# A fused decoder layer on eight cores: first weight slots used in turn over both chunks, and five pieces of work re-timed

## The reference

```
x = x + 1/2 * SwiGLU_1(RMSNorm(x))              # d_ff 2816: (silu(h@w1) * (h@w3)) @ w2
h = RMSNorm(x); proj = h @ w_in                 # q|k|v|gate r|decay code|pool u|ga|gb, 5648 columns
a = gated linear attention(q, k, v, decay)      # 4 heads, chunked, state dk 128 x dv 256
a = (RMSNorm per head(a) * silu(r)) @ w_up_a
b = (causal means of u over 2/4/8/16 tokens - u), 128x128 map per group, @ w_up_b
x = x + (sigmoid(ga) * a + sigmoid(gb) * b) @ w_mix_out
x = x + CrossAttention(RMSNorm(x), RMSNorm(mem))# 4 heads into 256 memory tokens
x = x + 1/2 * SwiGLU_2(RMSNorm(x))
out = RMSNorm(x)
```

## Time and profile before

| | us |
|---|---|
| median of 3 runs (lowest, highest) | 3164.24 (3163.45, 3164.89) |
| profiled execution, its own time | 3164.13 |
| span of its slowest core, core 3 | 3162.3 |
| shortest and longest core span | 3154.3, 3162.3 |
| TensorE busy | 3101.8 (98%) |
| VectorE, ScalarE, GpSimd busy | 1186.6, 950.2, 481.1 |
| DMA over the span | mean 92 GB/s |

### The profile page before, as it was taken

The page is one execution under the profiler, slowest core; times in us unless marked ns, Lnnn a source line. Parts: engine busy times, 40 slices in busy tenths (PEclk is TensorE's granted clock), DMA queues, the critical chain, the costliest instruction groups (busy, mean ns, idle before and its releaser), DMA issues.

```text
span 3162.3 us, 43137 instructions; the slowest of 8 cores (3154.3 to 3162.3 us)
## 1 busy us (share of the span) xinstructions
PE 3101.8 (98%) x15350; PEld 1448.9 (46%) x15350; DVE 1186.6 (38%) x1880; ACT 950.2 (30%) x1637; POOL 481.1 (15%) x557
## 2 busy tenths in 40 slices
PE   6999999999999999999999999999999999999998
PEld 2444454444444454444444445444444444544443
DVE  2231743621421373551332156363232226536212
ACT  3121442521211253252121135243212114425211
POOL 0002111220200220112110112012121021112002
PEclk9999999999999999999999999999999999999999
DMA  8597444335663534334384365232548345422534
GB/s 165 87 162 120 83 81 120 59 62 95 124 122 70 99 68 94 107 67 76 65 170 76 56 107 100 48 120 54 91 92 159 64 79 93 81 67 52 93 67 104
DMA packets 56784, 292.32 MB, mean 92 GB/s; under 512 B 5632, under 2 KB 11136, under 8 KB 32256
## 3 DMA queue, kind: packets, MB, share of 16 engines
q0 software_dynamic: 39024, 251.35, 44.5%
q1 hardware_dynamic: 17552, 38.21, 3.7%
HBM read 495.78 MB, written 22.02 MB: 164 GB/s over the span
## 4 chain that ended last, share of the span: by engine, by line
PE 94%; DVE 2%; DMA 2%; issue 1%; ACT 0%; SPq 0%; DVEq 0%; ACTq 0%; POOLq 0%; POOL 0%
PE psum_all L106 94%; DMA vo_s<-ov_mst 1%; PE psum_all L122 1%; DVE sb_hT L418 1%; DMA sb_small<-small 0%; DVE ov_nmx L1019 0%; DMA sb_slot<-ffn_w 0%; SPq L134 0%; DVE ov_Pm L1031 0%; DVE ov_pwA L733 0%; ACT ov_rstd L412 0%; DVE sb_xT L418 0%; ACT ov_rstd L410 0%; DVE ov_kT L700 0%; DVE ov_pwB L733 0%
## 5 line engine op out<-in xcount | busy, mean ns | idle before, releaser
L106 PE MATMUL psum_all<-sb_hT,sb_slot 128*128 128x512 bf16 x7680 | 1692.4, 380 | 9.0 <-DVE sb_hT L418 7.9
L106 PEld LDWEIGHTS psum_all<-sb_hT,sb_slot 128*128 128x128 bf16 x7680 | 749.8, 98 | 911.6 <-issue 23.9
L106 PE MATMUL psum_all<-ov_gated,sb_slot 128*128 128x512 bf16 x2816 | 613.2, 380 | 3.4 <-DMA sb_slot<-ffn_w 3.4
L518 DVE TENSOR_TENSOR ov_gated<-psum_all,ov_sl 128x512 bf16<-128x512 f32 x352 | 243.4, 692 | 924.0 <-PE psum_all L106 892.9
L515 ACT ACTIVATE ov_sl<-psum_all 128x512 bf16<-128x512 f32 x352 | 210.2, 597 | 902.8 <-PE psum_all L106 870.4
L106 PEld LDWEIGHTS psum_all<-ov_gated,sb_slot 128*128 128x128 bf16 x2816 | 276.0, 98 | 337.1 <-issue 6.1
L387 ACT ACTIVATE ov_sqt<-sb_xT 128x512 bf16<-128x512 f32 x224 | 140.1, 629 | 550.7 <-DVE sb_xT L539 215.8
L394 POOL TENSOR_TENSOR ov_acc<-ov_acc,ov_sqt 128x512 f32<-128x512 f32 x180 | 211.4, 1175 | 482.9 <-ACT ov_sqt L387 480.3
L134 POOL DMA_DIRECT2D sb_slot<-ffn_w x176 | 95.1, 542 | 1238.5 <-PE psum_all L106 1213.6
L106 PE MATMUL psum_all<-sb_slot,sb_hT 128*128 128x512 bf16 x1024 | 235.4, 379 | 2.6 <-DVE ov_kT L700 2.6
L418 DVE SCALAR_TENSOR_TENSOR sb_hT<-sb_xT,sb_small,ov_rstd 128x512 bf16<-128x512 f32 x192 | 141.7, 798 | 29.6 <-ACT ov_rstd L412 29.6
(11 more groups left out here) (138 smaller groups left out, 2007.7 us busy)
## 6 DMA issues: line engine op xcount, KB each, us to landing
sb_slot<-ffn_w POOLq DMA_DIRECT2D x88, 1024.0 KB, 11.2
sb_slot<-ffn_w POOLq DMA_DIRECT2D x88, 704.0 KB, 7.2
sb_slot<-w_in POOLq DMA_DIRECT2D x40, 1024.0 KB, 13.2
out<-sb_xT SPq DMA_DIRECT2D x14, 1024.0 KB, 11.9
ov_xin<-x SPq DMA_DIRECT2D x12, 1024.0 KB, 13.7
sb_slot<-w_up_a POOLq DMA_DIRECT2D x8, 1024.0 KB, 12.5
sb_slot<-w_mix_out POOLq DMA_DIRECT2D x8, 1024.0 KB, 11.2
sb_slot<-kq_s POOLq DMA_DIRECT2D x8, 1024.0 KB, 5.1
```

The source lines that it names most:

```text
L106: ("ins", (lambda e, o=o, l=l, r=r, st=st, sp=sp: e.matmul(o, l, r, start=st, stop=sp)), i == n - 1)
L518: S.op("dve", lambda e, b3=b3, slt=slt, j=j, s=s: e.tensor_tensor(out=gated[:, j, sl(s)], in0=b3[:], in1=slt[:], op=ALU.mult), [bb3, slb[0 ...
```

## The change

The staging tiles get a table of places, `MST_AT`: no tile lies at 98 or 99 any more, 55 and 56 come in, and those at 90 to 97 stand third to tenth in the order of use, not sixth to thirteenth (with 98 and 99 behind them). SP issues the constants ahead of x. The memsets of the ones matrices stand ahead of the two casts. POOL loads slot 0 once x's second piece is there, then x's second chunk with no wait, then slot 1. The memory's load waits for slot 1 and no longer for x's second chunk. In pass 1 of tile 0 the first pair is split into two single slots: chunk 0 and then chunk 1 go through slot 0, then both through slot 1, and the second chunk's norm comes after the first two column blocks, not the first four. The memory's squares come after chunk 1 of slot 1, and `mem_rest` is a step of its own that is emitted after column block 4. `pool(3 - i, 1)` takes the groups in the reverse order. In `xattn` a block's transposes stand a step later and between the two halves of a later block's scores; the last one stands behind the loop.

```diff
@@ -22,7 +22,8 @@
-NMST = 19
+MST_AT = [50, 51, 90, 91, 92, 93, 94, 95, 96, 97, 52, 53, 54, 46, 47, 48, 49, 55, 56]
+NMST = len(MST_AT)
@@ -291,7 +292,7 @@
-    mst = [ov(f"mst{i}", 50 + i if i < 5 else 85 + i if i < 15 else 31 + i, [128, 512], BF16) for i in range(NMST)]
+    mst = [ov(f"mst{i}", MST_AT[i], [128, 512], BF16) for i in range(NMST)]
@@ -350,14 +351,14 @@
         for lo in range(0, 8, step):
             S.dma(queue, [(xt[:, lo:lo + step, :], x_d[k, :, lo:lo + step, :])], after, xb[lo:lo + step], f"dma:x{queue}{k % 2}_{lo}")
 
+    S.dma("sp", [(small[:], small_d)], [], [const_b], "dma:const")
     load_chunk(0, 1)
-    S.dma("sp", [(small[:], small_d)], [], [const_b], "dma:const")
     wa_b = Buf("walpha")
     cb2 = Buf("const2")
+    S.op("dve", lambda e: e.memset(onesD[:], 1.0 / 1024.0), [], [cb2])
+    S.op("dve", lambda e: e.memset(onesV[:], 1.0 / 256.0), [], [cb2])
     S.op("dve", lambda e: e.tensor_copy(out=identB[:], in_=small[:, O_IDENT:O_IDENT + 128]), [const_b], [cb2])
     S.op("dve", lambda e: e.tensor_copy(out=triB[:], in_=small[:, O_TRI:O_TRI + 128]), [const_b], [cb2])
-    S.op("dve", lambda e: e.memset(onesD[:], 1.0 / 1024.0), [], [cb2])
-    S.op("dve", lambda e: e.memset(onesV[:], 1.0 / 256.0), [], [cb2])
     CB = [const_b, cb2]
 
     def gvec(off, kc):
@@ -492,9 +493,10 @@
     def ffn(l, x_in, hooks, nxt, between=(), drip=()):
         S.label = f"ffn{l}/p1"
         drip = list(drip)
-        pairs = [(0, 1), (2, 3), (4, 5), (6, 7), (8, 9), (10,)]
         between = list(between)
-        ahead = 0 if between else 1
+        first = len(between) > 0
+        pairs = ([(0,), (1,)] if first else [(0, 1)]) + [(2, 3), (4, 5), (6, 7), (8, 9), (10,)]
+        ahead = 0 if first else 1
         got = {}
         for pi, pair in enumerate(pairs):
             for jp in [jp for p in pairs[:pi + 1 + ahead] for jp in p]:
@@ -518,13 +520,13 @@
                         S.op("dve", lambda e, b3=b3, slt=slt, j=j, s=s: e.tensor_tensor(
                             out=gated[:, j, sl(s)], in0=b3[:], in1=slt[:], op=ALU.mult),
                             [bb3, slb[0]], [gb])
-                        if pi == 0 and s == 0 and between and j == 1:
+                        if s == 0 and j == 0 and first:
                             deferred.pop(0)()
-                        if s == 0 and j == (3 if between else 0):
+                        if s == 0 and j == (1 if first else 0):
                             run_deferred()
-                        if pi >= 1 and drip:
+                        if pi >= (2 if first else 1) and drip:
                             drip.pop(0)()
-                if (pi, s) >= (0, 1) and between:
+                if (pi, s) >= (1, 1) and between:
                     S.label = "mem"
                     between.pop(0)()
                     S.label = f"ffn{l}/p1"
@@ -917,7 +919,7 @@
             if i >= 3:
                 fill()
             if i < 4:
-                pool(i, 1)
+                pool(3 - i, 1)
             if i == 9:
                 pend["yb"] = xload(0, wpb_d, wpb_db)
                 pend["gb1"] = xload(1, win_d[10])
@@ -1056,7 +1058,10 @@
             hook(s, m + 1)
 
         for i in range(8):
-            scores_mm(i)
+            scores_mm(i, (0,))
+            if i >= 3:
+                transp(i - 3)
+            scores_mm(i, (1,))
             if i == 0:
                 S.label = "xa/dnorm"
                 n1.ones()
@@ -1067,8 +1072,7 @@
                 finish(i - 1)
             if i < 2:
                 n1.apply(4 * i, 4 * i + 4)
-            if i >= 2:
-                transp(i - 2)
+        transp(5)
         finish(7)
         ffn_pre(1)
         for m in range(8):
@@ -1084,13 +1088,14 @@
 
     S.label = "load"
     x0 = xin[0][1]
-    wpre(("ffn", 0, 0), w13_d[0][0], [xin[0][1][0]])
-    wpre(("ffn", 0, 1), w13_d[0][1], [xin[0][1][7]])
+    wpre(("ffn", 0, 0), w13_d[0][0], [xin[0][1][1]])
     load_chunk(1, 2, queue="pool")
+    wpre(("ffn", 0, 1), w13_d[0][1])
+    slot1 = pre_issued[("ffn", 0, 1)][1]
     x1 = xin[1][1]
     S.dma("pool", [(walpha[:], walpha_d), (wa[:], wa_d)], [], [wa_b], "dma:const2")
     S.dma("sp", [(pmf[:], pmix_d.rearrange("p (a b) -> p a b", a=4))], x1, pmf_b, "dma:pmf")
-    S.dma("sp", [(memT[:], mem_d)], x1, memT_b, "dma:mem")
+    S.dma("sp", [(memT[:], mem_d)], [slot1], memT_b, "dma:mem")
     n0 = first_norm(0, chain=0, raws=raw0)
     n0.sq_all()
     n0.rest()
@@ -1101,7 +1106,7 @@
         S.label = "ffn0"
         if t == 0:
             mb = mem_blocks()
-            mb = [mnorm.sq_all, lambda f=mb[0]: (mem_rest(), f())] + mb[1:]
+            mb = [mnorm.sq_all] + mb
         nx0, nx1 = xnorm(O_G_MIX, 0), xnorm(O_G_MIX, 1, chain=7)
 
         def nxt(idx):
@@ -1117,7 +1122,7 @@
         hooks = {(0, m): [lambda m=m, f=nx0: f.sq(m)] for m in range(8)}
         hooks.update({(1, m): [lambda m=m, f=nx1: f.sq(m)] for m in range(8)})
         hooks[(1, 6)].append(nx0.rest)
-        ffn(0, xin, hooks, nxt, mb if t == 0 else ())
+        ffn(0, xin, hooks, nxt, mb if t == 0 else (), [mem_rest] if t == 0 else ())
         n1 = mixer(t, nx1)
         n1 = xattn(t, n1)
         S.label = "ffn1"
```

## The result

The changed kernel takes 3143.91 us (median of five; its runs lie between 3142.49 and 3143.97) against 3164.89 for the kernel before in the same session (3163.45 to 3168.49): 21.0 us less, a ratio of 0.993 (95% interval 0.991 to 0.9945). A second session gave the same ratio, with medians of 3140.96 and 3163.0. The forecast was 3145.0. In some executions the cores of a die had a lower granted clock and took 50 us and more longer, and every range and ratio here leaves these out.

A forecast was written before the change was run, and what follows sets the result against it. TensorE, busy 98% of the span, bounds the kernel, so only its waits could be won. On core 7, 3161.7 - 6.5 - 9.4 - 3.1 + 0.5 = 3143.2, with 1.8 around it 3145.0 us; range 3139 to 3152.

The forecast's parts named there:

- start: Before and in tile 0's first matmuls: first matmul on slot 0 4.9 us earlier, plus 1.6 from pace; 6.5 less.
- memory's norm: At the first block on `mhT`: 7.2 us of TensorE idle and 2.2 of slow restart go; 9.4 less on every core.
- transposes: In `xattn`: the four waits for `Pm`, 0.9 and three times 0.7, go; 3.1 us less.
- poolings: Waits for `ogT` and `kT` in step 4 go (4.3 us), four bank waits of 1.2 come (4.8); 0.5 more.
- staging: At POOL's w2 load: core 3 gains 3.4 us plus 1.4 of slow restart, 4.8; core 7's 1.8 stays.
- The term for the pace: First eight matmuls on slot 0 come 0.43 us apart instead of 0.66: 7 x 0.23 = 1.6 us less.
- What would show it: Signs on the slowest core's trace, such as TensorE starting at 14 to 15 us and no waits for `mhT` or `Pm`.
- Rivals C: Memory's load or squares come late, so its norm still stops TensorE; 9.4 partly returns, 3150 to 3154 us; chance 0.07.
- D: Memory lands so late behind slot 1 that its ones matmuls wait; slower than before, 3165 to 3170 us; chance 0.03.
- Rival B: At the poolings: the bank wait is not met, all 4.3 us are gained, time 3140; chance 0.12.
- the sum: Core 7, forecast slowest: 3161.7 - 6.5 - 9.4 - 3.1 + 0.5 = 3143.2 us; core 3: 3139.0.
- rival A: At the start: x's last piece creeps while slot 0 streams; the start gives 0 to 1 us, 3151; chance 0.20.

The follow-up runs named there:

- the order 3, 0, 2, 1: Changed kernel with chunk 1's poolings taken as 3, 0, 2, 1, not 3, 2, 1, 0: median 3137.3 us, beside 3141.0 for the changed kernel.
- both slots first: Changed kernel with poolings 3, 0, 2, 1 and chunk 0 through slots 0 and 1 before chunk 1: median 3131.2 us, beside the changed kernel's 3141.0.

## Why the prediction was right

**The mechanism of each part held, and only sizes were off.** As differences from the kernel before by the ratios, on the slowest core: start 8.2 (forecast 6.5), memory's norm 9.5 (9.4), transposes 3.8 (3.1), poolings 0.6 less with an interval from 4 less to 2.5 more (0.5 more), staging 1.3 less with an interval from 5 less to 3 more (nothing, since core 7's wait stays). They add up to 23.4, and the whole change gave 21.0 and 22.1. The parts are thus additive to what can be told, which is not finely: each of these intervals is 6 us wide or more.

**Start, 8.2 instead of 6.5.** Both terms were too small. The first matmul came 5.5 (core 7) and 5.9 us (core 3) earlier, against 4.9. The term for the pace was 1.6, the difference of 0.66 and 0.43 over seven matmuls, as if the rest of the restart were equally slow in both kernels. It was not: only the first six matmuls come 0.43 apart now, and full clock is granted in the whole first block. From its first matmul on slot 0 to the second chunk's ones matmuls, core 3 took 18.48 us for 64 before and 8.32 for 32 now; at the warm 0.216 a matmul (10.36 for 48) that is 4.7 and 1.4 lost, so 3.3 is won. Of this 0.4 goes back in the second norm (6.39 from its ones matmuls to the restart instead of 5.95), and 0.7 in the 112 matmuls behind it, which lose 5.1 where 128 lost 4.4: after this restart the granted clock stays at half for 8.7 us, and before it was back after 7.3. 5.9 + 3.3 - 0.4 - 0.7 = 8.1. The prediction had put this second norm at nothing won or lost.

**What would show it.** TensorE's first instruction was forecast at 14 to 15 and came at 6.8 to 11.2. That was a slip, not a finding: each ones matmul waits for its own piece, so the first goes with the first square. Only the last mattered, and it ended at 14.7 on core 7. The first matmul on slot 0, forecast at 22.3, came at 21.7 to 23.2, and on the slowest core it waited for the DMA, as forecast. No wait of over 5 us appeared before 70 us but those ahead of the first block.

**Memory's norm, as forecast.** The apply of `mhT` ended at 73.91 on core 3, 3.2 us before TensorE asked for it, and no bank ran out:

```profile
69.31 4.60 DVE L419 SCALAR_TENSOR_TENSOR ov_mhT<-sb_memT,sb_small,ov_rstd 128x256 bf16<-128x256 f32 x8 [2.44 <-ACT ov_rstd L413]
```

The memory landed 14.9 us after its issue on core 7, at 50.6, where I had taken the 22.4 of the earlier trace rows and 61; the ones matmuls came at 65.6 there and at 65.8 on core 3. Rivals C and D had no part in it.

**Poolings, as forecast.** The bank was the same one: four new waits of 1.08 against the 1.2 of the prediction, 4.3 for the 4.3 that went. A shifted sum's 0.80 from start to start was the right price. Rival B asked for this wait not to be met; it is met in every tile, and the order 3, 0, 2, 1 shows what B would have given, 3.6 us.

**The slowest core: the sum was right, the core wrong.** Core 7 was to come out at 3143.2 and came out at 3134.3. It lost 18.5 by the sum, 1.7 more at the start and 0.5 at the poolings, and 4.7 of waits for loads which I had left in place: 5.3 before, the 1.8 of the earlier trace rows and four for `w_in`, of which 0.6 is left. The four, in the kernel before on that core:

```profile
PE psum_all L106 <- DMA sb_slot<-w_in: 3.5, 4, 1.1
```

With 2.0 us that no term explains that is its 27.4. The late loads now stand on core 2, and they move between executions: in the next run of the changed kernel core 2 had a span of 3132.6 and core 3 one of 3140.0. So the time of the slowest core could be forecast from core 7 as if its load waits stayed, since in each profile of the changed kernel some core loses time to late DMAs, while the core itself could not. That the number came within 1.1 us is in part luck, by two errors that cancel: core 7 gave 8.9 us more than its sum, and core 2, which stood at 3155.8 before, gave only 13.8. In the second profile it is x's late last piece on core 5, rival A on one core, that fills the place of the late loads.

## What to carry to other kernels

A saved wait at the start was worth more than its length, since the restart behind it was shorter too: let the applies run ahead while a load is still under way, and the matmuls then start in a close row. When one load is released by the arrival of another's first pieces, the margin differs from core to core and from execution to execution, so look at all cores of more than one profile. When a chain of small operations stops TensorE, look for independent work of its length and move it in between, and then check which load or buffer is waited for next; here that was worth 9.4 us at the memory's norm and 3.5 at the second chunk's. Moving elementwise work out of one step costs in the step that takes it as soon as its engine has no gap left there, so spread the long ones apart instead of bringing them all forward.

## What the hardware showed beyond this

- A few hundred nanoseconds at the start decide 8 us. With slot 0 issued at x's first piece, core 5 issues it at 6.42 and squares the last piece of x at 23.66; core 0 issues it at 6.71 and squares the last at 15.44. In between lies only whether x's 2 MB have nearly passed when POOL's packets begin to take every other turn.
- Why the granted clock fell where it did stays open. On core 3 of the changed kernel it stayed at 1.00 through the stop of 6.6 us ahead of slot 0's block, and fell inside the shorter one, which lasts from 32.8 to 36.57:

```profile
34.00:35.00 1.00, 0.00 (x0) 0.00 (x0) 0.00 (x0) 0.90 (x3) 0.00 (x0) 1.00 1.25 217
35.00:36.00 1.00, 0.00 (x0) 0.00 (x0) 0.33 (x1) 0.50 (x1) 0.00 (x0) 0.50 1.13 193
```

  It came back at 45.2. With both slots first, on core 2, it fell at 36.0, 0.3 us after a restart in a close row, and came back at 39.4. So neither the length of a stop nor the pace behind it tells where it falls. A granted clock of 1.00 does not mean full pace either: on core 7 six weight loads of the first block come 0.43 apart up to 24.2, and the next 24 take 5.06 us.
- The memory's load of 1 MB on SP's queue took 14.4 us on core 3 of the changed kernel (14.9 on core 7) and 22.4 on core 3 before, with loads of POOL beside it both times. What it met on the way was not taken apart.
